# Order and pairing of the GLA output products in a one-core decoder step

## The chip, the cores and the metric

The kernel runs on one core of one Trainium2 chip. The metric is the device time of one execution in microseconds. A core has five engines that matter here: PE (TensorE, matmuls; its weight loads are shown as PEld), ACT (ScalarE), DVE (VectorE), POOL (GpSimd) and SP (SyncE, which here only issues DMAs). Each engine works through its own queue in order, and the engines wait for one another through semaphores.

## What is computed

One decoder layer for a prompt of 512 tokens and 8 sequences of 4 sample tokens, all in fp32: a gated linear attention (GLA) group and a sliding-window attention group side by side, one output projection, a layer norm, a mixture of 32 experts (top 4), a second layer norm. The part that matters here is the output of GLA, which the reference computes by chunks:

```
def step(S, inp):
    qi, ki, vi, gi = inp
    b = jnp.cumsum(gi, axis=2)
    b_last = b[:, :, -1:, :]
    o_inter = jnp.einsum('bhtd,bhde->bhte', qi * jnp.exp(b), S)
    diff = jnp.where(causal[:, :, None], b[:, :, :, None, :] - b[:, :, None, :, :], -jnp.inf)
    att = jnp.einsum('bhtd,bhtsd,bhsd->bhts', qi, jnp.exp(diff), ki)
    o = o_inter + jnp.einsum('bhts,bhse->bhte', att, vi)
    ...
o_gla = rms_norm_f32(o_gla, gla_norm_g) * jax.nn.silu(o_gate ...)
mix = jnp.concatenate([o_gla, o_swa], axis=-1) @ w_out
x1 = layer_norm(DEEPNORM_ALPHA * x + mix, ln1_g, ln1_b)
```

There are 4 heads with keys of 64 and values of 128. The output of a chunk is the sum of the scores times the values (within the chunk) and of the decayed queries times the state that the chunks before left.

## The kernel before

The tokens lie in five tiles: tiles 0 to 3 are 128 prompt tokens each (the kernel's chunk is a tile), tile 4 holds the 32 sample tokens. The stages follow one another: projections, attention, the seven "levels" that build the GLA score matrices attT (L1010 on PE, L2097 on DVE), the chunk states (L1030 and L2122), the GLA outputs, their normalisation and gating, the mixer transposes and the output projection (L1116, L1120), layer norm and routing, and then the 32 experts (L1205, L1208), whose weights stream through a ring of 16 slots.

PSUM is used as four units of two banks each. Every intermediate result has a name and a unit (ORDER), and a name can be written only after the name before it on the same unit has been freed. For the stage of the change: go0 (the output of tile 0) is on unit 0, go1 on unit 1, go2 on unit 2, go3 on unit 0 again, go4 (the samples) on unit 3. After them mixT0 is on unit 0, mixT1 on unit 1, out0 on unit 2. The output of head h = 2a + q lies in bank q of the unit, at column a * 128.

The GLA outputs on PE (L1080 to L1097). For tiles 0 to 3 and heads 0 to 3: a product of attT with gv (128 rows, 128 columns, L1088), and for tiles 1 to 3 directly behind it the product of the queries qe with the state of the tile before (L1090), into the same place. A head's keys take 64 rows, so qe and state of heads with q = 0 are in rows 0 to 63 of the array and those with q = 1 in rows 64 to 127. The samples' last products (L1095, 32 rows and 32 columns) come after tile 3. Each fp32 matmul appears as two records in the profile.

Behind PE, ACT takes the tiles in the order 0, 1, 2, 3, 4: four squares with sums (L1656) and a root (L1660). DVE follows (norm_gate, L2165): a reciprocal (L2170), four products with the gate (L2176); then it frees the unit and raises mix_ready. PE's mix_T(0) (L741 through the helper transposes) waits for mix_ready 1 and for unit 0, which is free after norm_gate(3). ACT copies the transposes (L1368, tile mix_a), and out_product(0) (L1116) follows.

SP's queue around it: ln_b is loaded after level6, the residual rows res[:, 2:] and res of the samples after go4 (L517 to L519), since res shares its memory with gv; the weights of the first expert wait for mix_ready 5 and for all earlier output DMAs. DVE reads res first in L2198, after out0. The order on each engine is written out by hand; there is no planner.

Of the kernel before, what the change touches and what calls it, by code (L numbers as in the profile page):

```python
# [21 lines left out]
P = 128  # L22
D = 1024
KD = D // P
HALF = 512
# [4 lines left out]
PT = SEQ // P  # L30
NT = PT + 1
GH, GDK, GDV = 4, 64, 128
# [85 lines left out]
def build(nc, d):  # L118
    with ExitStack() as ctx:
        def sem(name):  # L120
            return ctx.enter_context(nc.semaphore(name))
# [7 lines left out]
        def sb(name, shape, dt=F32):  # L129
            size = 2 if dt == BF16 else 4  # L130
            for n in shape[1:]:
                size *= n
            t = nc.alloc_sbuf_tensor_at(name, shape, dt, offset=here[0])
            here[0] += (size + 31) // 32 * 32
            return t
# [56 lines left out]
        gv = sb("gv", [P, NT, 512])  # L192
# [48 lines left out]
        state = sb("state", [P, PT, 2, GDV])  # L241
# [21 lines left out]
        attT = sb("attT", [P, 16, P])  # L263
# [23 lines left out]
        qe = sb("qe", [P, 2, T])  # L287
# [68 lines left out]
        def c_(name):  # L356
            a, n = early_at[name]
            return ce[:, a:a + n]
# [11 lines left out]
        def filled(name):  # L370
            return full[USE[name][0]], USE[name][1] + 1

        def emptied(name):
            return freed[USE[name][0]], USE[name][1] + 1
# [4 lines left out]
        def s_full(name):  # L379
            return full[USE[name][0]]  # L380
# [4 lines left out]
        def bank(name):  # L385
            return unit[USE[name][0]]
# [22 lines left out]
        def s_room(name):  # L409
# [23 lines left out]
        state_ready, sstate_ready, s_read, s_decayed, rms_ready, mix_ready = (sem(n) for n in (  # L433
            "state_ready", "sstate_ready", "s_read", "s_decayed", "rms_ready", "mix_ready"))
# [44 lines left out]
        def _(sp):  # L479
# [3 lines left out]
            for n in range(NIN):  # L483
# [14 lines left out]
                if 1 <= n <= 3:  # L498
                    i = n + 1
# [15 lines left out]
            sp.wait_ge(*filled("level6"))  # L515
            sp.dma_start(ln_b[:], d["ln1_b"].partition_broadcast(P)).then_inc(ln_in, 16)
            sp.wait_ge(*filled("go4"))  # L517
            sp.dma_start(res[:, 2:PT], d["x_prompt"][0, 2 * P:SEQ].rearrange("(i p) d -> p i d", p=P)).then_inc(res_in, 16)
            sp.dma_start(res[:NS, PT], d["x_sample"].rearrange("n t d -> (n t) d")).then_inc(res_in, 16)  # L519

# [210 lines left out]
        def _(pe):  # L731
            mm, tr = nc.tensor.matmul, nc.tensor.transpose
# [257 lines left out]
            for i in range(NT):  # L990
                name = f"qkT{i // 2}"
# [3 lines left out]
                for c in range(4):  # L995
                    at = i % 2 * HALF + c * r
                    ins = tr(bank(name)[:, at:at + r], qk[:r, i, c * P:(c + 1) * P], ident[:r, :r])
# [36 lines left out]
            def sample_out(a, q):  # L1034
                return bank("go4")[:NS, q * HALF + a * GDV:q * HALF + (a + 1) * GDV]
# [41 lines left out]
            level(5)  # L1077
            level(6)
            pe.wait_ge(att_ready, 1)
            for i in range(PT):  # L1080
                name = f"go{i}"
                pe.wait_ge(*emptied(name))
                if i:
                    pe.wait_ge(state_ready, i)
                for h in range(GH):
                    a, q = divmod(h, 2)
                    out = bank(name)[:, q * HALF + a * GDV:q * HALF + (a + 1) * GDV]
                    ins = mm(out, attT[:, q * 8 + a * PT + i], gv[:, i, h * GDV:(h + 1) * GDV], start=True, stop=i == 0)  # L1088
                    if i:
                        ins = mm(out, qe[64 * q:64 * q + 64, a, i * P:(i + 1) * P], state[64 * q:64 * q + 64, i - 1, a],  # L1090
                                 start=False, stop=True)
                ins.then_inc(s_full(name), 1)
            for h in range(GH):
                a, q = divmod(h, 2)
                ins = mm(sample_out(a, q), attS[:, q * 2 + a], gv[:NS, PT, h * GDV:(h + 1) * GDV], start=False,  # L1095
                         stop=a == 1)
            ins.then_inc(s_full("go4"), 1)  # L1097

            def mix_T(i):
                def src(k):  # L1100
                    return (og[:rows(i), i, k * P:(k + 1) * P] if k < 4
                            else qkv[:rows(i), i, (k - 4) * P:(k - 3) * P])
                pe.wait_ge(mix_ready, i + 1)
                if i == PT:
                    pe.wait_ge(selo, 1)
                transposes(f"mixT{i}", src, i)
# [54 lines left out]
            for b in range(PT):  # L1161
                ins = mm(bank("pos")[:, (b + 1) * NE:NT * NE].rearrange("p (t e) -> p t e", e=NE), c_("ones"),
                         msk[:, b:b + 1].to_broadcast([P, PT - b, NE]), start=False, stop=b == PT - 1)
            ins.then_inc(s_full("pos"), 1)
            pe.wait_ge(*emptied("count"))
            for i in range(NT):
                ins = mm(bank("count")[:NE, 0:1], msk[:, i], c_("ones")[:, 0:1], start=i == 0, stop=i == NT - 1)
# [164 lines left out]
            with pe.If(n_extra > 0):  # L1332
                with pe.Fori(0, MAXEXTRA) as j:
                    with pe.If(j < n_extra):
# [3 lines left out]
                        for k in range(KD):  # L1338
                            ins = tr(px[:, k * P:(k + 1) * P], xg[:, k * P:(k + 1) * P], ident)
# [3 lines left out]
                        for a, (out, lhs) in enumerate(((pg, xeTx), (pu, xeTx), (pd, heTx))):  # L1343
                            if a == 2:
                                pe.wait_ge(v_dve, j * 4 + 4)
                                for k in range(KD):
                                    ins = tr(px[:, k * P:(k + 1) * P], hbx[:, k * P:(k + 1) * P], ident)
# [3 lines left out]
                            for h in range(2):  # L1351
# [3 lines left out]
                                for k in range(KD):  # L1355
                                    ins = mm(out[:, cols], lhs[:, k], raw_x[:, k, cols], start=a == 2 and k == 0,
                                             stop=k == KD - 1)
# [1194 lines left out]
```

## Time and profile before

| | us |
|---|---|
| median of 3 runs | 1500.42 |
| lowest, highest | 1498.47, 1500.81 |
| the profiled execution | 1500.29 |
| its span, first to last instruction | 1498.1 |
| PE busy in the span | 1410.9 (94%) |
| DVE busy | 471.2 (31%) |
| ACT busy | 322.8 (22%) |
| mean granted TensorE clock | 0.952 |

Times in the rows are in us from the span's start. An engine is called busy while an instruction of it runs; records of PE may overlap, so a group's mean duration is longer than the step from one start to the next. The granted clock is a share of 2.4 GHz: 1.00 is 2.4 GHz and 0.50 is 1.2 GHz. The chain of waits is followed back from the last instruction, at each step to what released it.

### The profile page before, as it was taken

Reading aid. Unit: us, or ns where it says so; the run is one execution under the profiler, and the core shown is the slowest. Engines: PE = TensorE matmul, PEld = TensorE weight load, DVE = VectorE, ACT = ScalarE, POOL = GpSimd, SP = SyncE. Lnnn points to the kernel's source line nnn. Section 1 sums busy time; section 2 is a strip of 40 time slices with the busy share of each in tenths; the row PEclk is TensorE's granted clock in tenths of the full one; section 3 lists DMA queues with packets and bytes.
Section 4 is the critical chain, followed back from the end, with each engine's and each line's share of the span. In section 5 each row is a group of like instructions: output and inputs, shape, how many; then the busy total and the mean of one; then the engine's idle time right before and its main releaser. Section 6 shows DMA issues by size and latency. Waiting matters only on the chain.

```text
span 1498.1 us, 37690 instructions
## 1 busy us (share of the span) xinstructions
PE 1410.9 (94%) x16570; PEld 962.2 (64%) x16570; DVE 471.2 (31%) x895; ACT 322.8 (22%) x662; POOL 115.8 (8%) x119
## 2 busy tenths in 40 slices
PE   6999967998899999999999999999999999999991
PEld 5777756555566666666666666666666666666660
DVE  3235546237432222222223223222222222222223
ACT  3544453203111111112111111111111111121114
POOL 1022000000110100000100000001000000000000
PEclk8999986698799999999999999999999999999996
DMA  7211050426699999999999999999999999999944
GB/s 239 87 47 57 1 187 24 157 123 236 247 377 388 399 390 392 402 398 399 397 387 399 396 392 399 397 400 400 392 391 399 390 395 399 399 398 399 384 183 141
DMA packets 78468, 463.93 MB, mean 310 GB/s; under 512 B 12400, under 2 KB 13632, under 8 KB 29008
## 3 DMA queue, kind: packets, MB, share of 16 engines
q1 hardware_dynamic: 67616, 429.54, 72.0%
q0 software_dynamic: 10192, 31.31, 8.2%
q8 instruction: 132, 2.16, 0.6%
q10 hardware_dynamic: 512, 0.79, 0.1%
q14 instruction: 16, 0.13, 0.0%
HBM read 444.70 MB, written 22.22 MB: 312 GB/s over the span
## 4 chain that ended last, share of the span: by engine, by line
PE 87%; DVE 4%; ACT 3%; PEld 2%; DMA 2%; issue 2%; DVEq 0%; POOL 0%; PEldq 0%; SPq 0%; ACTq 0%; POOLq 0%
PE unit L1205 41%; PE unit L1208 26%; PE unit L1116 4%; PE unit L1188 2%; PE unit L1193 2%; PE unit L746 1%; PE unit L748 1%; PE unit L747 1%; PE unit L741 1%; PE unit L1010 1%; DMA xbuf<-x_prompt_dram 1%; PE unit L1088 1%; DVE attT L2097 1%; PE unit L1090 1%; PEld unit L898 1%
## 5 line engine op out<-in xcount | busy, mean ns | idle before, releaser
L1205 PE MATMUL unit<-ring_b,xeT 128*32 128x512 f32 (+1 forms) x3168 | 354.5, 489 | 1.1 <-ACT xeT L1368 1.1
L1208 PE MATMUL unit<-ring_b,xeT 128*32 128x256 f32 x1584 | 355.0, 382 | 0.0
L1208 PE MATMUL unit<-ring_a,xeT 128*32 128x256 f32 x1488 | 330.7, 379 | 0.0
L1205 PE MATMUL unit<-ring_a,xeT 128*32 128x256 f32 (+1 forms) x2976 | 330.2, 486 | 0.0
L1208 PEld LDWEIGHTS unit<-ring_b,xeT 128*32 128x32 f32 x1584 | 171.7, 110 | 56.5 <-issue 1.2
L1208 PEld LDWEIGHTS unit<-ring_a,xeT 128*32 128x32 f32 x1488 | 161.8, 110 | 52.5
L1208 PE MATMUL unit<-ring_a,heT 128*32 128x256 f32 x768 | 169.7, 379 | 0.0
L1205 PE MATMUL unit<-ring_a,heT 128*32 128x512 f32 (+1 forms) x1536 | 169.4, 486 | 0.0
L1205 PEld LDWEIGHTS unit<-ring_b,xeT 128*32 128x32 f32 x3168 | 126.8, 110 | 60.9 <-issue 5.0
L1208 PE MATMUL unit<-ring_b,heT 128*32 128x256 f32 x720 | 160.3, 379 | 0.0
L1205 PE MATMUL unit<-ring_b,heT 128*32 128x256 f32 (+1 forms) x1440 | 160.1, 486 | 0.0
L1205 PEld LDWEIGHTS unit<-ring_a,xeT 128*32 128x32 f32 x2976 | 120.2, 110 | 51.7 <-issue 2.5
L1368 ACT ACTIVATE heT<-unit 128x768 f32<-128x768 f32 x31 | 25.2, 812 | 509.7 <-PE unit L1193 509.7
L2373 DVE TENSOR_TENSOR hb<-unit,brow 128x768 f32<-128x768 f32 x32 | 30.7, 958 | 305.0 <-PE unit L1208 305.0
L2343 DVE TENSOR_TENSOR gm<-unit,brow 128x768 f32<-128x768 f32 x32 | 30.7, 958 | 234.8 <-PE unit L1208 234.8
L1208 PEld LDWEIGHTS unit<-ring_a,heT 128*32 128x32 f32 x768 | 84.3, 110 | 27.1
L683 POOL DMA_INDIRECT acc_rows<-ysb,idx x32 | 46.6, 1456 | 683.8 <-ACT ysb L1753 672.6
L1208 PEld LDWEIGHTS unit<-ring_b,heT 128*32 128x32 f32 x720 | 79.2, 110 | 25.4
L1749 ACT ACTIVATE ysb<-unit,gcol 96x768 f32<-96x768 f32 x32 | 28.7, 898 | 250.2 <-PE unit L1208 250.2
L1205 PEld LDWEIGHTS unit<-ring_a,heT 128*32 128x32 f32 x1536 | 62.9, 110 | 28.9 <-issue 0.9
L1205 PEld LDWEIGHTS unit<-ring_b,heT 128*32 128x32 f32 x1440 | 59.2, 110 | 27.9
L2273 DVE TENSOR_TENSOR row_part<-unit,ck 96x3 f32<-96x3 f32 x32 | 5.0, 156 | 209.4 <-PE unit L1182 209.4
(319 smaller groups left out, 1635.0 us busy)
## 6 DMA issues: line engine op xcount, KB each, us to landing
ring_b<-w_gate_dram SPq DMA_DIRECT2D x68, 1024.0 KB
ring_a<-w_down_dram SPq DMA_DIRECT2D x68, 1024.0 KB
ring_b<-w_up_dram SPq DMA_DIRECT2D x64, 1024.0 KB
ring_a<-w_up_dram SPq DMA_DIRECT2D x64, 1024.0 KB
ring_a<-w_gate_dram SPq DMA_DIRECT2D x60, 1024.0 KB
ring_b<-w_down_dram SPq DMA_DIRECT2D x60, 1024.0 KB
raw_a<-w_in_dram SPq DMA_DIRECT2D x16, 512.0 KB, 3.6
wo<-w_out_dram SPq DMA_DIRECT2D x4, 1024.0 KB, 12.3
```

The source lines that it names most:

```text
L683: return pool.indirect_dma_start(acc_dram, bass.IndirectOffsetOnAxis(ap=at, axis=0), out, None, compute_op=ALU.add)
L741: ins = tr(bank(name)[:, k * r:(k + 1) * r], src(k), ident[:r, :r])
L746: mm(out, xh, wh, start=start, stop=False)
L1116: ins = mm(bank(name)[:, h * HALF:(h + 1) * HALF], mix[i % 2][:, k], wo[:, k, h * HALF:(h + 1) * HALF], start=k == 0, stop=k == KD - 1)
L1188: ins = tr(px[:, k * P:k * P + CAP], half, ident[:CAP, :CAP])
L1193: ins = tr(px[:, k * P:(k + 1) * P], gm[:, k * P:(k + 1) * P], ident)
L1205: return mm(out[j * NS:(j + 1) * NS, a:b], stat(j), w[:, a:b], start=first, stop=last)
L1208: return mm(out[CAP:P, j * 256:(j + 1) * 256], stat(j), w[:, FOLD:D], start=start, stop=stop)
L1368: copy = lambda out, src, scale=1.0: nc.scalar.activation(out, src, ACT.Copy, scale=scale)
L1749: nc.scalar.activation(ysb[:CAP, 0:FOLD], pd[:CAP, 0:FOLD], ACT.Identity, scale=gcol[:CAP, par:par + 1])
L2343: tt(gm[:], pg[:, 0:FOLD], brow[:, 0], ALU.add).then_inc(h_part, 1)
L2373: tt(hb[:], pu[:, 0:FOLD], brow[:, 1], ALU.add).then_inc(h_part, 1)
```

## The change

The outputs of a tile are split into two functions. within_chunk(i) does the four score products of a tile, bank by bank (q outside, a inside), with start only for the first product of a bank. from_state(i) does the four state products, with q inside, so that the two row halves alternate. PE runs within_chunk of tiles 0, 1 and 2, then the samples' products, then from_state(1) and (2), then within_chunk(3) and from_state(3). SP waits for go3 as well before it loads res[:, 2:].

```diff
             sp.wait_ge(*filled("go4"))
+            sp.wait_ge(*filled("go3"))
             sp.dma_start(res[:, 2:PT], d["x_prompt"][0, 2 * P:SEQ].rearrange("(i p) d -> p i d", p=P)).then_inc(res_in, 16)
...
             pe.wait_ge(att_ready, 1)
-            for i in range(PT):
-                name = f"go{i}"
-                pe.wait_ge(*emptied(name))
-                if i:
-                    pe.wait_ge(state_ready, i)
-                for h in range(GH):
-                    a, q = divmod(h, 2)
-                    out = bank(name)[:, q * HALF + a * GDV:q * HALF + (a + 1) * GDV]
-                    ins = mm(out, attT[:, q * 8 + a * PT + i], gv[:, i, h * GDV:(h + 1) * GDV], start=True, stop=i == 0)
-                    if i:
-                        ins = mm(out, qe[64 * q:64 * q + 64, a, i * P:(i + 1) * P], state[64 * q:64 * q + 64, i - 1, a],
-                                 start=False, stop=True)
-                ins.then_inc(s_full(name), 1)
+            def head_out(i, a, q):
+                return bank(f"go{i}")[:, q * HALF + a * GDV:q * HALF + (a + 1) * GDV]
+
+            def within_chunk(i):
+                pe.wait_ge(*emptied(f"go{i}"))
+                for q in range(2):
+                    for a in range(2):
+                        h = 2 * a + q
+                        ins = mm(head_out(i, a, q), attT[:, q * 8 + a * PT + i], gv[:, i, h * GDV:(h + 1) * GDV],
+                                 start=a == 0, stop=i == 0 and a == 1)
+                if i == 0:
+                    ins.then_inc(s_full("go0"), 1)
+
+            def from_state(i):
+                pe.wait_ge(state_ready, i)
+                for a in range(2):
+                    for q in range(2):
+                        ins = mm(head_out(i, a, q), qe[64 * q:64 * q + 64, a, i * P:(i + 1) * P],
+                                 state[64 * q:64 * q + 64, i - 1, a], start=False, stop=a == 1)
+                ins.then_inc(s_full(f"go{i}"), 1)
+
+            within_chunk(0)
+            within_chunk(1)
+            within_chunk(2)
             for h in range(GH):
                 a, q = divmod(h, 2)
                 ins = mm(sample_out(a, q), attS[:, q * 2 + a], gv[:NS, PT, h * GDV:(h + 1) * GDV], start=False,
                          stop=a == 1)
             ins.then_inc(s_full("go4"), 1)
+            from_state(1)
+            from_state(2)
+            within_chunk(3)
+            from_state(3)
```

## Rows read from the trace of the kernel before

**Rows 1.** The page: the chain that ended last, share of the span by engine.
```profile
PE 87%; DVE 4%; ACT 3%; PEld 2%; DMA 2%; issue 2%; DVEq 0%; POOL 0%; PEldq 0%; SPq 0%; ACTq 0%; POOLq 0%
```

**Rows 2.** Stretch, length, busy us of PE, PEld, DVE, ACT, POOL, clock, DMA, GB/s.
```profile
1000.00:1400.00 400.00, 400.00 (x5390) 267.68 (x5386) 101.54 (x179) 62.53 (x108) 30.62 (x24) 1.00 1.02 396
```

**Rows 3.** Waits of SP's queue, 380 to 1480: total us, times, longest.
```profile
SPq L532 <- PE unit L1208: 866.1, 367, 32.0
```

**Rows 4.** Chain of waits in order of time around the change: start, us, what.
```profile
264.58 2.50 PE unit L1088 x10
267.09 0.72 PE unit L1090 x2
267.81 0.72 PE unit L1088 x2
...
283.76 1.15 ACT squares L1656 x8
...
285.17 0.19 DVE ms L2170
...
286.72 0.03 DVEq L2180
...
290.04 13.87 PE unit L1116 x32
```

**Rows 5.** Busy time by stretch, columns as in rows 2: where the clock moved.
```profile
228.06:231.47 3.41, 3.41 (x29) 2.37 (x30) 3.12 (x5) 1.06 (x1) 0.00 (x0) 0.50 0.00 0
231.47:234.70 3.23, 3.23 (x60) 3.04 (x56) 2.69 (x7) 0.00 (x0) 0.00 (x0) 1.00 0.03 5
...
241.71:245.12 3.41, 0.00 (x0) 0.00 (x0) 2.80 (x6) 3.41 (x4) 0.59 (x1) 1.00 0.00 0
...
245.92:264.58 18.66, 11.62 (x112) 10.84 (x112) 8.04 (x11) 0.00 (x0) 1.17 (x1) 0.50 0.27 79
264.58:285.56 20.98, 20.98 (x64) 14.89 (x64) 4.19 (x17) 6.68 (x37) 0.00 (x0) 0.50 0.03 11
286.79:289.50 2.71, 2.71 (x13) 2.71 (x14) 1.98 (x7) 0.88 (x2) 0.00 (x0) 0.50 0.84 301
289.50:303.70 14.20, 14.20 (x37) 6.44 (x36) 0.07 (x1) 1.32 (x2) 0.00 (x0) 1.00 1.02 413
...
388.49:395.31 6.82, 5.77 (x43) 2.53 (x45) 1.13 (x1) 2.18 (x3) 2.12 (x3) 0.50 0.40 119
```

**Rows 6.** Timeline of PE: start, us from first start to last end, instruction.
```profile
230.78 0.83 PE L1048 MATMUL unit<-s,qbm 64*32 64x128 f32 x6
249.53 3.68 PE L1010 MATMUL unit<-qR,kE 64*128 64x64 f32 x32
264.58 2.50 PE L1088 MATMUL unit<-gv,attT 128*128 128x128 f32 x10 [2.80 <-DVEq L2112]
283.65 1.91 PE L1095 MATMUL unit<-gv,attS 32*32 32x128 f32 x8
```

**Rows 7.** Single lines: durations in ns (min/median/max), first and last start.
```profile
L1048 PE MATMUL unit<-s,qbm x6: 401/418/418, 230.8 to 231.2; 64*32 64x128 f32 x6
L1088 PE MATMUL unit<-gv,attT x32: 421/421/582, 264.6 to 282.6; 128*128 128x128 f32 x32
```

**Rows 8.** Timeline of all engines, tile 0's normalisation to the first transposes.
```profile
269.68 1.12 DVE L2176 SCALAR_TENSOR_TENSOR og<-unit,ms,og 128x128 f32<-128x128 f32 x4
...
272.19 0.28 ACT L1656 ACTIVATE squares<-unit 128x128 f32<-128x128 f32 x1 [2.83 <-PE unit L1090]
...
273.36 0.21 ACT L1660 ACTIVATE ms<-ms 128x4 f32<-128x4 f32 x1
...
283.76 0.28 ACT L1656 ACTIVATE squares<-unit 128x128 f32<-128x128 f32 x1 [4.41 <-PE unit L1090]
...
286.79 1.09 PE L741 MATMUL unit<-ck,og 128*128 128x128 f32 x4 [1.23 <-DVEq L2180]
```

## The prediction

> **What bounds the kernel now.** First the page's chain by engine, then the busy time of the expert stage. PE carries 87% of the chain [rows 1]. From 1000 to 1400 us, a stretch of it, PE is busy throughout [rows 2], while the weight queue on SP waits for PE to free ring slots, 866.1 us in 367 waits [rows 3]. The experts are bound by PE, not by DMA, and nothing in them is touched here: they stay as they are and start when what is before them ends. Then the chain around the change, in order of time [rows 4]. It passes without a gap through the GLA outputs: ten L1088 records (scores), then two L1090 (states) and two L1088 in turn, 0.72 us for each two; then ACT's squares and root and DVE's normalisation of tile 3, the mixer transposes L741, the output products L1116. From 264.58 to 283.74 that stage is PE's, and a granted clock of 0.50 stands over all of it [rows 5], which is 1.2 of 2.4 GHz. It rose only at 289.50. So PE is the bound, and a slow one, for two reasons besides the clock.
>
> **Reason one, the alternation.** At 1.2 GHz a back to back record of 128 columns costs 0.213 us: L1095's 8 records take 1.91 us, the last of them, like every such record, 0.42, and (1.91 - 0.42) / 7 = 0.213 [rows 6, 7]. A matmul is two records. One full alternation (two L1088, two L1090) takes 2 x 0.72 = 1.45 us [rows 4], against 4 x 0.213 = 0.85; the other 0.60 are two changes between 128 and 64 rows, 0.30 each. The stage's 64 records at 0.213 are 13.6, its 24 changes at 0.30 are 7.2: 20.8, where 20.98 is measured from the first start to L1095's end [rows 5], so the account is whole.
>
> **Reason two, one row half at a time.** L1048 has 64 rows and 128 moving columns as L1090 has, but takes both row halves in turn. Six of its records at 1.2 GHz take 0.83 us, each 0.418 long: two steps of 0.206 for three pairs [rows 6, 7]. So the halves run side by side, 0.107 a record at L1095's step. Its stationary side has 32 columns where L1090 has 128. L1010 has 128 and also goes through the halves in turn: 32 records in 3.68 us, 0.115 a record with start and end [rows 6], but only 64 moving columns. One row bounds the moving side, one the loading side; none has both wide. If loads and moving hide each other, a pair costs 0.213, and that I take, since L1088 loads 128 columns under 128 moving at (2.50 - 0.58) / 9 = 0.213 after its first record [rows 6, 7]. The other end is 0.213 a record, halves one after another.
> Here the Trainium skill (TensorE: Matmul & The Clock Gate, Part 3, "The mechanism") speaks against the change: it says that a weight load overlaps running matmuls only where the row groups differ. By that the next pair's loads would lie behind the running one, an estimated 0.32 a pair and 1.3 us more for 12 pairs; L1088 disagrees in this trace, for each of its loads uses the same rows as the matmul before it.
>
> **The change part by part**, in us of the profiled execution.
> (1) within_chunk(0), (1), (2) run back to back: 24 records, the first step longer (0.58 against 0.42 of duration), then 0.213 each; at the low clock the last starts at 269.65. The zeroing of a bank is now done by the first product in it; same instructions, no cost. Tile 0 is filled at 266.7 as before.
> (2) The samples' 8 records follow, with one change before and one behind.
> (3) from_state(1), (2): 8 pairs, no change between them. Then a change, within_chunk(3), a change, from_state(3), 4 pairs.
> Sum at the low clock: 24 changes become 4, 20 x 0.30 = 6.0 off; 24 state records go from 0.213 to 0.107, 2.6 off; 20.98 becomes 12.4. go3, filled at 283.7 now with the samples behind it, is filled at about 277.3 with the samples ahead of it.
> (4) The clock. It rose at 231.47 under L1043 and L1048, at 289.50 after 2.71 us of back to back 128x128 transposes, and at 395.31, 5.4 us after the first expert product at 389.89; neither the half-wide L1010 nor the alternation brought it [rows 5]. The change makes a back to back stretch of 128x128 products of 5.3 us. I take it that the clock rises within it or at its end, 2.7 to 5.4 us after its start, and work with 269.0. The remaining steps halve: samples until 270.5, go1 filled at 271.2, go2 at 271.7, within_chunk(3) from 271.8, go3 at 273.5. within_chunk(3) needs unit 0 free of tile 0; norm_gate(0) ends at 269.68 + 1.12 = 270.8 [rows 8], just in time, and that would be felt (under 1 us) if tile 3 stood earlier in the order.
> (5) What is late next. mix_T(0) writes unit 0, so it waits for norm_gate(3). ACT takes the tiles in order; one costs it 1.38 (272.19 to 273.57 [rows 8]) and DVE 1.55 (285.17 to 286.72 [rows 4]). Both have idled between tiles (ACT 4.41 before the last squares [rows 8]); now they queue. go1 at 271.2, ACT until 272.6, then DVE has three tiles in a row: 272.7 + 3 x 1.55 = 277.4. L741 starts at 277.4 instead of 286.79: **9.4 us** off. With a rise at 267.3 or at 270.0 the same walk gives 10.3 or 8.6.
> (6) PE's idle gap before L741 grows from 1.23 [rows 8] to 3.9 us. In 241.71 to 245.12 PE was idle throughout and the clock fell [rows 5]. If it falls here too, the transposes and ACT's copy take the same 3.15 us as now, and a late rise lets some L1116 records cost 0.86 instead of 0.43: 0 to 1.5 lost. If it stays, 16 transposes take 1.7 instead of 3.25, of which 0.85 shows, the rest being under ACT's copy of the first eight. I book zero, between the two.
> The Trainium skill (TensorE: Matmul & The Clock Gate, "Why this matters for your kernels") warns that PE gaps over about 3 us between bursts bring back the low clock. By that rule the time is up to 1.5 us over mine.
> (7) SP. The loads of res[:, 2:] and of the samples' rows must not overwrite gv, so they now wait for go3 as well: 273.5, where they waited for the samples until 285.56 (283.65 + 1.91 [rows 6]). Behind them in SP's queue stands the expert weight stream, which waits for mix_ready = 5 anyway; norm_gate(4) ends 1.5 after norm_gate(3), so it starts some 9 us earlier too. The first reader of res is L2198, which waits for out0, the 13.87 us of L1116 behind L741 [rows 4]. Cost nothing; if the stream did not move, it would only lose slack.
> (8) Behind L1116 every gate up to the experts is PE, DVE, ACT or a DMA that one of them releases; none stands at a fixed time. The 9.4 us arrive at the end.
>
> **The sum.** The profiled execution took 1500.29 (its span of 1498.1 and 2.2 around it), 0.13 under the median of 1500.42, so its differences are taken over as they are: 1500.42 - 9.4 = **1491.0**.
>
> **The rivals.**
> A, the forecast: 10.3 + 0.85 to 8.6 - 1.5 off, 1489.3 to 1493.3. 64%.
> B, the clock stays low through the stage, as now. For it: the 11.62 us of PE work on 64 and 32 rows within 245.92 to 264.58 did not raise it [rows 5]; against it: the new stretch is as dense as the transposes that did. go3 at 277.3, then ACT and DVE as now (283.74 to 286.79, 3.05): 280.35, 6.4 off, 1494.0. 15%.
> C, the halves do not run side by side where both sides are 128 wide. With a risen clock go1 comes 0.4 later and the rest hides under DVE: 1491.4, inside A. With the low clock 2.6 come on top of B: 1496.6. 5%.
> D, better than all that: under 1489.3, by an early rise and the clock's phase later on. 5%.
> E, the saving is returned before the experts. The clock is low in 388.49 to 395.31 [rows 5], under 5.4 us of the first expert product; where its rise falls can differ by one to two us either way, and only on top of B or C does that bring the result within 0.2% of now, 1497.4 and more. 8%.
> F, slower: the clock falls in the new gap and stays low under the output products. At twice its 0.43 (13.87 / 32 [rows 4]), an L1116 record loses 0.43; 9.4 + 3.0 us are lost after 29 records, some 25 us at the low clock. The longest dense run at the low clock here, from 389.89, is 5.4 us. 1503.4 and more. 3%.
>
> **How the numbers follow.** The range goes from just under A to C's end, 1488.0 to 1496.6, and leaves out about one in eight. 0.2%, 3.0 us, is about what a measurement of this kernel can tell from no change. Faster: A, B, C and D, 0.89; same 0.08; slower 0.03.
>
> **What would show it.** In the profile after: records of the score products at 0.21, then 0.11 us; four steps of 0.3 where there were 24; state records starting two by two; a rise of the clock between 267.3 and 270.0; ACT and DVE without idle time between tiles 1, 2 and 3; L741 at about 277.4; L1205 some 9 us earlier. Wrong would be: a clock of 0.50 throughout (then 1494.0), state records one by one, L741 released by something other than norm_gate(3), or a longer expert stage.

## The result and the profile after

| | before | changed |
|---|---|---|
| median, 4 runs each (us) | 1499.99 | 1491.52 |
| lowest to highest | 1498.47 to 1500.81 | 1489.86 to 1491.93 |
| profiled execution | 1500.29 | 1491.93 |
| its span | 1498.1 | 1489.8 |

The ratio is 0.9943, 95% interval 0.9927 to 0.9959: 8.5 us less, where 9.4 were forecast. A second set of four runs of the same program, taken later beside other variants, gave 1491.20 and 0.9940 (0.9924 to 0.9957).

In the changed kernel the lines have moved: scores L1091 (was L1088), states L1101 (was L1090), samples L1110 (was L1095), transposes L742, output products L1135, squares L1675, DVE's reciprocal and gating L2189 and L2195, experts L1224 and L1227. First the timeline of PE through the stage (start, us from first start to last end), which answers to rows 4 and 6:

```profile
264.61 5.49 PE L1091 MATMUL unit<-gv,attT 128*128 128x128 f32 x24 [2.80 <-DVEq L2131]
270.03 1.29 PE L1110 MATMUL unit<-gv,attS 32*32 32x128 f32 x8
271.25 1.16 PE L1101 MATMUL unit<-state,qe 64*128 64x128 f32 x16
272.34 1.16 PE L1091 MATMUL unit<-gv,attT 128*128 128x128 f32 x8
273.43 0.71 PE L1101 MATMUL unit<-state,qe 64*128 64x128 f32 x8
278.35 1.09 PE L742 MATMUL unit<-ck,og 128*128 128x128 f32 x4 [4.20 <-DVEq L2199]
```

The stage that took 20.98 us takes 9.53 (264.61 to 274.14). Then PE is idle for 4.20 us, where it was idle for 1.23 [rows 8]. The busy time by stretch shows the clock (last but two column), as rows 5 did:

```profile
270.54:274.14 3.60, 3.60 (x39) 2.95 (x37) 0.90 (x5) 2.10 (x16) 0.00 (x0) 1.00 0.00 0
274.14:277.36 3.22, 0.00 (x1) 0.00 (x0) 2.52 (x11) 2.92 (x22) 0.00 (x0) 1.00 0.56 172
277.36:278.35 0.99, 0.01 (x1) 0.04 (x1) 0.78 (x4) 0.00 (x0) 0.00 (x0) 0.50 0.97 401
278.35:284.19 5.84, 5.84 (x19) 4.45 (x20) 2.05 (x7) 2.05 (x2) 0.00 (x0) 0.50 0.55 215
```

It rose at 270.54, fell at 277.36 in the gap and rose again only at 284.19, 2.4 us into the output products. The chain of waits, which answers to rows 4, shows what the stage is bound by now:

```profile
270.10 1.22 PE unit L1110 x8
271.32 0.67 PE unit L1101 x8
272.01 1.15 ACT squares L1675 x8
...
273.42 0.19 DVE ms L2189
...
273.71 1.14 DVE og L2195 x4
...
275.07 0.19 DVE ms L2189
...
276.73 0.19 DVE ms L2189
...
278.35 3.65 PE unit L742 x16
281.99 14.89 PE unit L1135 x32
```

PE is in it only until tile 1 is filled, at 272.0; from there, behind ACT's squares of tile 1, DVE normalises three tiles in a row, 1.65 us each (273.42, 275.07, 276.73). out0 takes 14.89 where it took 13.87 [rows 4]. The expert stage is as it was, PE busy throughout and SP waiting for it, 866.4 us in 367 waits [rows 2, 3].

```profile
1000.00:1400.00 400.00, 400.00 (x5394) 267.93 (x5389) 102.43 (x179) 62.43 (x108) 30.38 (x24) 1.00 1.02 395
...
SPq L533 <- PE unit L1227: 866.4, 367, 31.0
```

### The profile page after: what moved, and what is told of

Its sections match the earlier page's. It is cut to its first block, busy times and chain, and to the rows that moved or that the text cites. A ratio compares the mean times of both kernels' runs of the same rounds, so it can differ in the third digit from the quotient of the medians.

```text
span 1489.8 us, 37688 instructions
## 1 busy us (share of the span) xinstructions
PE 1402.5 (94%) x16570; PEld 959.1 (64%) x16570; DVE 471.1 (32%) x895; ACT 322.2 (22%) x662; POOL 114.8 (8%) x119
## 4 chain that ended last, share of the span: by engine, by line
PE 87%; DVE 4%; ACT 3%; DMA 2%; PEld 2%; issue 2%; DVEq 0%; SPq 0%; POOL 0%; PEldq 0%; ACTq 0%; POOLq 0%
PE unit L1224 41%; PE unit L1227 26%; PE unit L1135 4%; PE unit L1207 2%; PE unit L1212 2%; PE unit L747 1%; PE unit L749 1%; PE unit L748 1%; PE unit L1011 1%; PE unit L742 1%; DMA xbuf<-x_prompt_dram 1%; PE unit L1153 1%; PEld unit L899 1%; DVE attT L2116 1%; PE unit L875 0%
## 5 line engine op out<-in xcount | busy, mean ns | idle before, releaser
L1224 PE MATMUL unit<-ring_b,xeT 128*32 128x512 f32 (+1 forms) x3168 | 353.9, 489 | 1.1 <-ACT xeT L1387 1.1
L1227 PE MATMUL unit<-ring_b,xeT 128*32 128x256 f32 x1584 | 354.5, 382 | 0.0
L1227 PE MATMUL unit<-ring_a,xeT 128*32 128x256 f32 x1488 | 330.7, 380 | 0.0
L1224 PE MATMUL unit<-ring_a,xeT 128*32 128x256 f32 (+1 forms) x2976 | 330.2, 486 | 0.0
L1227 PEld LDWEIGHTS unit<-ring_b,xeT 128*32 128x32 f32 x1584 | 172.0, 111 | 56.3 <-issue 1.0
L1227 PEld LDWEIGHTS unit<-ring_a,xeT 128*32 128x32 f32 x1488 | 162.2, 110 | 52.4
L1227 PE MATMUL unit<-ring_a,heT 128*32 128x256 f32 x768 | 169.7, 379 | 0.0
L1224 PE MATMUL unit<-ring_a,heT 128*32 128x512 f32 (+1 forms) x1536 | 169.4, 486 | 0.0
L1224 PEld LDWEIGHTS unit<-ring_b,xeT 128*32 128x32 f32 x3168 | 126.8, 110 | 60.4 <-issue 4.5
L1227 PE MATMUL unit<-ring_b,heT 128*32 128x256 f32 x720 | 160.3, 379 | 0.0
L1224 PE MATMUL unit<-ring_b,heT 128*32 128x256 f32 (+1 forms) x1440 | 160.1, 486 | 0.0
L1224 PEld LDWEIGHTS unit<-ring_a,xeT 128*32 128x32 f32 x2976 | 120.3, 110 | 51.4 <-issue 2.5
L1227 PEld LDWEIGHTS unit<-ring_a,heT 128*32 128x32 f32 x768 | 84.5, 110 | 27.0
L1227 PEld LDWEIGHTS unit<-ring_b,heT 128*32 128x32 f32 x720 | 79.4, 110 | 25.3
L1224 PEld LDWEIGHTS unit<-ring_a,heT 128*32 128x32 f32 x1536 | 63.0, 110 | 28.7 <-issue 0.9
L1224 PEld LDWEIGHTS unit<-ring_b,heT 128*32 128x32 f32 x1440 | 59.3, 110 | 27.8
```

The lines of the kernel that those rows point to most:

```text
L1224: return mm(out[j * NS:(j + 1) * NS, a:b], stat(j), w[:, a:b], start=first, stop=last)
L1227: return mm(out[CAP:P, j * 256:(j + 1) * 256], stat(j), w[:, FOLD:D], start=start, stop=stop)
```

## The experiments

The theory: the stage gained by fewer changes of row count, by row halves side by side and by the clock, and DVE's queue of three tiles and the gap ahead of L742 took part of it back. The rivals were that the halves do not matter, that the clock is no matter of what PE does here, and that the order (24 score records, 12 products, together, samples in between, tile 3 last) is what brings the gain. All ratios are to the kernel before on the same chip: its median was 1499.99 beside the changed kernel, 1500.48 beside the halves in blocks, tile by tile, samples last and other units, 1499.34 beside the other units with samples last or tile by tile, the doubled scores and the halves apart, 1500.06 beside the rest. So medians from different groups are compared by their ratios. The last two columns are read from each profile: from the first score product to the first mixer transpose, and to the first output product.

| kernel | median (us) | ratio (95%) | to transposes | to out0 |
|---|---|---|---|---|
| before | 1499.34 to 1500.48 | 1 | 22.2 | 25.4 |
| changed | 1491.52 | 0.9943 (0.9927 to 0.9959) | 13.7 | 17.2 |
| changed, second set | 1491.20 | 0.9940 (0.9924 to 0.9957) | 13.3 | 16.7 |
| halves in blocks | 1490.09 | 0.9932 (0.9915 to 0.9948) | 13.3 | 16.8 |
| tile by tile | 1488.65 | 0.9921 (0.9904 to 0.9937) | 11.5 | 14.7 |
| samples last | 1489.80 | 0.9930 (0.9913 to 0.9946) | 12.0 | 15.5 |
| other units | 1487.60 | 0.9915 (0.9899 to 0.9932) | 10.0 | 13.2 |
| other units, samples last | 1487.30 | 0.9917 (0.9901 to 0.9934) | 9.4 | 12.6 |
| other units, tile by tile | 1486.38 | 0.9914 (0.9898 to 0.9931) | 9.1 | 11.9 |
| the same, copy first | 1486.32 | 0.9908 (0.9892 to 0.9925) | 9.5 | 11.8 |
| other units on before | 1498.87 | 0.9992 (0.9982 to 1.0002) | 20.9 | 24.4 |
| doubled scores on before | 1497.04 (one run) | | 18.8 | 22.2 |
| halves apart | 1492.87 (one run) | | 15.2 | 18.4 |
| tile 3 early | 1492.41 (one run) | | 14.5 | 18.0 |

**Row halves in blocks.**

```diff
-                for a in range(2):
-                    for q in range(2):
+                for q in range(2):
+                    for a in range(2):
                         ins = mm(head_out(i, a, q), qe[...], state[...], start=False, stop=a == 1)
```

> The changed kernel with the state products of one row half after the other (q outside, a inside). If row halves run side by side where both sides are 128 wide (theory A), the state records stop starting in pairs: at the clock of 2.4 GHz a record then costs about 0.107 us instead of 0.053, so go1 is filled some 0.4 us later (272.4), the transposes L741 start at about 278.8 and the time is 0.4 us over the changed kernel, about 1491.9, not to be told from it by the time but by the starts. If the pairs give nothing (theory C), starts and time are as in the changed kernel, 1491.5.

The timeline of PE shows the 16 state records in 1.26 us, where the changed kernel has 1.16:

```profile
268.83 1.26 PE L1101 MATMUL unit<-state,qe 64*128 64x128 f32 x16
...
L1101 PE MATMUL unit<-state,qe x8: 272/272/373, 268.8 to 269.3; 64*128 64x128 f32 x8
```

I expected 1.7 or more (16 x 0.107) under theory A. The second row, of the single line, has 8 records starting within 0.5 us (by their starts in pairs, 0.01 us apart), although the program has four of one half and then four of the other. So this edit did not do what it was made for: the order within from_state decides nothing, PE takes up the other half over four records. The time (1490.09) is not over the changed kernel's. Whether the halves matter was still open.

**Row halves apart.** The half with q = 0 of tiles 1 and 2 is put ahead of within_chunk(3), the half with q = 1 behind it. half_state(i, q) is from_state(i) for one q alone.

```diff
...
-            from_state(1)
-            from_state(2)
-            within_chunk(3)
-            from_state(3)
+            half_state(1, 0)
+            half_state(2, 0)
+            within_chunk(3)
+            half_state(1, 1)
+            half_state(2, 1)
+            half_state(3, 1)
+            half_state(3, 0)
```

> The changed kernel, with the state products of heads with q = 0 of tiles 1 and 2 (8 records, one row half) before within_chunk(3), and those with q = 1 behind it, then tile 3. Theory A (halves run side by side, and PE finds the other half among the next few records whatever their order): with none of the other half in reach, records of one half start one by one, 0.107 to 0.11 us apart at 2.4 GHz, twice the 0.053 of the changed kernel. Rival (a 64-row record of this size costs half anyway): 0.055 apart. The time, about 1.5 us over the changed kernel through the later go1, is not the question.

Timeline of PE, then the rows of the single line in that stretch, loads and matmuls (durations in ns, first and last start):

```profile
270.33 1.16 PE L1100 MATMUL unit<-state,qe 64*128 64x128 f32 x8
...
L1100 PEld LDWEIGHTS unit<-state,qe x8: 183/188/188, 270.3 to 271.1; 64*128 64x128 f32 x8
L1100 PE MATMUL unit<-state,qe x8: 272/272/373, 270.3 to 271.2; 64*128 64x128 f32 x8
```

Eight records of one half take the 1.16 us that sixteen take in the changed kernel. With 0.272 for the last and 0.214 for the first step, (1.16 - 0.27 - 0.21) / 6 = 0.113 a record against 0.053 in pairs. In this kernel the other half always goes to another PSUM bank too, but a change of bank alone does not make pairs: the first four of the eight records go to tile 1's unit and the next four to tile 2's, and the steps stay at 0.11. Theory A holds: halves run side by side with 128 columns loaded and 128 moving, and what the program must give is records of the other half close behind, not an alternation. How close, the 16 records behind within_chunk(3) bound: twelve of q = 1, then four of q = 0. Their first nine start one by one, 0.11 us apart, and pairs (0.005 us apart) come only among the last seven. The rows also weigh against what the Trainium skill says of loads (TensorE: Matmul & The Clock Gate, Part 3, "The mechanism"), that they overlap running matmuls only where row groups differ: these loads, each 0.18 to 0.19 long at steps of 0.11, use the same half of the rows as the matmul running, and the step is no longer than that of the 128-row L1091 (0.11). The same section also lets a load run ahead into a background weight buffer; that would fit the row, and no run here shows whether it is the reason.

**Scores twice, on the kernel before.** 12 score products (24 records) whose results are overwritten go ahead of the old loop.

```diff
             pe.wait_ge(att_ready, 1)
+            for name in ("go0", "go1", "go2"):
+                pe.wait_ge(*emptied(name))
+            for n in range(3):
+                for h in range(GH):
+                    a, q = divmod(h, 2)
+                    mm(bank(f"go{n}")[...], attT[:, q * 8 + a * PT + n], gv[:, n, ...], start=True, stop=True)
```

> The kernel before with the 12 score products of tiles 0 to 2 computed once more ahead of its loop (their results are overwritten), 24 back to back records and 5.3 us more work. Theory (dense products bring the clock up, the alternation did not): the clock rises in or just behind the added stretch, an alternation of four records takes about 0.85 us instead of 1.45, the 12 of them give back about 7 us, and the transposes run high: 1497 to 1499. Rival (the clock at this place does not depend on what PE does, or falls back under the alternation): 5.3 us more, 1505.5.

Busy time by stretch, and one of the chain's pairs of records:

```profile
264.05:268.46 4.41, 4.41 (x20) 4.41 (x21) 0.00 (x0) 0.00 (x0) 0.00 (x0) 0.50 0.16 51
268.46:279.71 11.25, 11.25 (x63) 8.35 (x61) 3.91 (x15) 5.32 (x28) 0.00 (x0) 1.00 0.00 0
...
270.20 0.42 PE unit L1097 x2
```

More work, and 2.3 us less time than the kernel before on that chip (1497.04 in one run, against 1499.10 to 1499.60 in seven). The clock rises under the added dense records and stays up through 11 us of the same alternation that ran low before; a cycle of four records takes 0.83 us instead of 1.45 [rows 4]. So the alternation does not bring the rise, but it does not bring a fall either; the clock fell at 282.12, in the idle gap of 2.08 us ahead of L741. A back to back record steps by 0.112 us at 2.4 GHz (0.113 by the row of the halves apart). Of the 0.83, 4 x 0.112 = 0.45 are the records and 0.38 the two changes: a change costs 0.19 at 2.4 GHz, 0.30 at 1.2.

**Tile by tile.** The split products in the old order of tiles, samples last.

```diff
-            within_chunk(1)
-            within_chunk(2)
+            for i in range(1, PT):
+                within_chunk(i)
+                from_state(i)
             for h in range(GH):
                 ...
-            from_state(1)
-            from_state(2)
-            within_chunk(3)
-            from_state(3)
```

> The split and paired products, but tile by tile as before: scores of tile 0, then scores and states of tiles 1, 2 and 3 each, the samples last. 6 changes of row count between the tiles' products instead of 24. Theory A (what counts is when the last tile comes and how ACT and DVE queue): go1 is filled at about 269.7, DVE does not queue three tiles in a row, and with a clock that rises in the stretch L741 starts at about 276.5, some 1.5 to 2 us before the changed kernel: 1489.5. Rival (the clock rises only because 24 score records stand together): it stays at 1.2 GHz, go3 is filled at about 275.9, L741 at 278.9 and the time is 1492.

```profile
264.84 3.78 PE L1091 MATMUL unit<-gv,attT 128*128 128x128 f32 x16 [2.80 <-DVEq L2128]
268.55 1.23 PE L1101 MATMUL unit<-state,qe 64*128 64x128 f32 x8
269.71 1.17 PE L1091 MATMUL unit<-gv,attT 128*128 128x128 f32 x8
...
273.19 1.05 PE L1111 MATMUL unit<-gv,attS 32*32 32x128 f32 x8
276.33 0.85 PE L742 MATMUL unit<-ck,og 128*128 128x128 f32 x4 [2.09 <-DVEq L2196]
```

This is PE's timeline. Theory A: L742 at 276.3 (276.5 expected), 1488.65 (1489.5 expected; its interval meets the changed kernel's, so the marks in the profile are what tells them apart). Tile 1 is filled at 269.8 instead of 272.0, while PE still runs low, and the clock rises all the same (eight records of L1091 take 1.17 us, as they do high). 24 score records need not stand together, and tile 3's place needs no care: PE comes to it at 271.45, when the wait for unit 0 is over. The clock still fell, at 276.60, just behind the remaining gap of 2.09 us: out0 is 14.7 us behind the start, 3.2 behind the transposes' start.

**Samples last.** The samples' products go behind from_state(3), nothing else.

> The changed kernel with the samples' products behind tile 3. By the account of the changed kernel (go1 at 272.0 sets ACT, then three tiles of 1.65 us on DVE) go1 comes 1.1 us earlier and so does L741, at about 277.2; PE's gap before it shrinks from 4.2 to about 2 us, so the clock may stay up and out_product(0) starts high, another 1 to 2 us: 1488.5 to 1490.5. If the place of the samples does not matter: 1491.5.

```profile
268.31 1.16 PE L1101 MATMUL unit<-state,qe 64*128 64x128 f32 x16
269.73 1.16 PE L1091 MATMUL unit<-gv,attT 128*128 128x128 f32 x8 [0.25 <-DVEq L2198]
...
271.46 1.06 PE L1114 MATMUL unit<-gv,attS 32*32 32x128 f32 x8
275.41 1.09 PE L742 MATMUL unit<-ck,og 128*128 128x128 f32 x4 [2.90 <-DVEq L2199]
```

Transposes start 12.0 us after the stage does, against 13.7 and 13.3: the samples in between cost the place that they take ahead of tile 1. Now within_chunk(3) does wait for unit 0, 0.25 us. The clock fell in the gap here too. The median of 1489.80 agrees, but its interval meets that of the changed kernel; the marks in the profile are what shows it.

**Tile 3 early.** within_chunk(3) ahead of from_state(1).

> The changed kernel with within_chunk(3) ahead of from_state(1). PE reaches it at about 271.2, after tile 0's unit is free (270.8), so there is no stall; but go1 is filled 1.1 us later and with it DVE's queue of three tiles and L741: 1 us over the changed kernel, 1492.5, seen in the profile as squares of tile 1 at about 7.5 + 1.0 us after the stage's start. If norm_gate(0) came later than PE, there would be an idle stretch of PE ahead of it.

```profile
270.76 1.16 PE L1091 MATMUL unit<-gv,attT 128*128 128x128 f32 x8 [0.34 <-DVEq L2198]
271.85 1.61 PE L1101 MATMUL unit<-state,qe 64*128 64x128 f32 x24
278.95 1.08 PE L742 MATMUL unit<-ck,og 128*128 128x128 f32 x4 [5.49 <-DVEq L2199]
```

PE did stall, 0.34 us, which the expectation had at none, since here it came sooner (the clock rose 4.4 us after the stage's start, not 5.9). Tile 3's place is worth that stall and the records ahead of tile 1: transposes at 14.5 us after the start, some 1 us later.

**Other units behind the stage.** The first 20 names after go4 take their PSUM unit in another turn.

```diff
-         + [(name, n % 4) for n, name in enumerate(TAIL)]
+         + [(name, (1, 2, 0, 3)[n % 4] if n < 20 else n % 4) for n, name in enumerate(TAIL)]
```

> The changed kernel with other PSUM units for what follows: mixT0 on unit 1, mixT1 on unit 2, out0 on unit 0, and so on in that turn for the first 20 names behind go4. The first transposes then wait for norm_gate(1) and (2) instead of (3). If the remaining gap of 4.2 us is only the wait for unit 0: L741 starts at about 275.0 and 276.7, the clock stays at 2.4 GHz, L1135's successor (output product of tile 0) starts at 278.4 instead of 281.8 and loses no 1.0 us to a low clock: 4.4 us under the changed kernel, 1487.1. If the gap has another cause or is returned later: 1491.5.

```profile
273.33 0.71 PE L1101 MATMUL unit<-state,qe 64*128 64x128 f32 x8
274.94 0.63 PE L742 MATMUL unit<-ck,og 128*128 128x128 f32 x4 [0.90 <-DVEq L2199]
...
276.59 0.63 PE L742 MATMUL unit<-ck,og 128*128 128x128 f32 x4 [0.59 <-DVEq L2199]
...
278.15 14.00 PE L1135 MATMUL unit<-wo,mix_a 128*128 128x512 f32 x32 [0.50 <-DVEq L2198]
```

The gap of 4.20 us is now three of 0.90, 0.59 and 0.50, the clock holds (four transposes in 0.63 us instead of 1.09, out0 in 14.00 instead of 14.89), and the first output product starts 13.2 us after the stage does instead of 17.2. 1487.60, 1487.1 expected. The gap was the wait for unit 0. The ratios' intervals just meet (0.9932 and 0.9927); the marks do not.

**The same units, samples last.**

> The other PSUM units for what follows, and the samples' products behind tile 3. Theory (DVE's queue of three tiles, started by go1, now sets the first output product): go1 comes 1.1 us earlier than with the units alone, norm_gate(3) ends at about 277.0 and the output product of tile 0 starts there: 1 us under the kernel with the units alone, 1486.6. If ACT (squares of tiles 1 to 3 and the samples, then the copy) sets it: no gain, 1487.6.

It starts out0 at 12.6, 0.6 earlier instead of 1.1, by DVE's queue as before; the clock of this profile rose late (the 24 score records take 5.49 us, so all of them were low). The times can't be told apart, by ratio 0.9917 and 0.9915.

**The same units, tile by tile.**

> The other PSUM units, and the products tile by tile with the samples last. ACT and DVE are fed in time, so norm_gate(3) ends at about 276.3, but ACT is done with the samples' squares only at 275.9 and copies the first transposes until 277.0: output product of tile 0 at 277.0, 1.2 us under the kernel with the units alone: 1486.4. If it is the same as that one (1487.6), something else releases the product.

```profile
271.87 1.06 PE L1111 MATMUL unit<-gv,attS 32*32 32x128 f32 x8
272.85 0.66 PE L742 MATMUL unit<-ck,og 128*128 128x128 f32 x4
...
275.65 13.97 PE L1132 MATMUL unit<-wo,mix_a 128*128 128x512 f32 x32 [0.83 <-ACT mix_a L1384]
```

PE's timeline: the transposes follow the samples without a gap, and the output product is released by ACT's copy, as expected. It starts 11.9 us after the stage does, 1.3 earlier than with the units alone. The time does not show it: 1486.38 is the number expected, but the kernel before was 1.1 us faster on this chip too, and the ratios are 0.9914 and 0.9915.

**The copy ahead of the samples' squares on ACT.** The squares and root of tile 4 move behind mix_in(0).

```diff
             mix_in(0)
+            rms(PT)
             mix_in(1)
```

> Products tile by tile, the other PSUM units, and on ACT the copy of the first transposes ahead of the samples' squares and root. If ACT's order sets the first output product, it now starts when norm_gate(3) is done on DVE, about 11.2 us after the stage's start instead of 11.9: 1485.7. If not: 1486.4.

```profile
274.93 0.20 ACT L1676 ACTIVATE ms<-ms 128x4 f32<-128x4 f32 x1
275.75 1.02 ACT L1384 ACTIVATE mix_a<-unit 128x1024 f32<-128x1024 f32 x1 [0.62 <-PE unit L742]
```

No gain to be measured: 1486.32, ratio 0.9908 against 0.9914, out0 at 11.8. ACT now idles 0.62 us for the transposes, which stand behind the samples on PE; in this profile the bound has gone back to PE. But here the clock rose 5.20 us after the stage's start, against 4.34 in the profile it is compared with, and so the transposes started 0.4 us later on PE (9.5 against 9.1). What ACT's order is worth with an equal clock stays open.

**The units alone, on the kernel before.**

> The kernel before with only the other PSUM units for what follows the GLA outputs. Theory (in the kernel before PE is behind on its own work, so the wait for unit 0 is worth little): transposes start when the samples end, at 285.6, the output product of tile 0 at about 289.0 instead of 289.9: 1 us less, 1499. Rival (the units are worth the 4 us that they are worth on top of the change): 1496.

```profile
283.32 1.84 PE unit L1095 x8
285.16 3.60 PE unit L741 x16
```

The transposes follow the samples at once; out0 starts 24.4 us after the stage does instead of 25.4, as expected. In time the ratio is 0.9992 (0.9982 to 1.0002), 1.2 us less and not told from no change, but well short of the rival's 4 us. The units are worth 4 us only where PE is ahead of DVE.

**The changed kernel again**, on the chip of the tile 3 early, copy first and units on before runs.

> The changed kernel once more, beside the runs below on the same chip: 1491.5, and 1490 to 1492.5 for single runs, whose spread comes from where the clock happens to rise and fall.

1491.20, with single runs from 1490.45 to 1491.83.

## Why the prediction was right, and what was off

The mechanism held: fewer changes, halves side by side, the clock, and DVE's queue as the next bound. That the median came within 0.5 us of 1491.0 is in part luck. By the saving it was 0.9 off, 8.5 against 9.4: the sum started from 1500.42, where the four runs of the kernel before have 1499.99. And in the profile 1.0 us less than forecast was saved at L742 and 1.4 more were lost in the gap and the low clock behind it; 0.6 and 0.5 that the forecast did not have came back later.

**What bounds, and the account of the stage** were right. Two changes and four records make the cycle of 1.45, and the experiment with doubled scores separates its parts again at the other clock.

**(1) to (3)** were right as far as the clock stayed low: 24 score records in 5.49 us, as the forecast's 5.07 to the last start and 0.42 have it. Four changes are left, three of them at the high clock. One slip in the sum: 264.58 + 12.4 gives 277.0 for go3 at the low clock, not 277.3; only rival B and its 1494.0 hang on it, by 0.3 us.

**Row halves** ran side by side, 16 records in 1.16 us at 2.4 GHz, 0.053 each. I wrote this as a merit of q inside a; the experiment with blocks shows that the inner order is worth nothing and the one with halves apart that their nearness is.

**(4), the clock,** rose as forecast, but at 270.54, 5.9 us after the start, while I had 4.4 and a range of 2.7 to 5.4, so it fell outside the range. Over the profiles in which it rose in the stage, it rose 4.3 to 5.9 us after the start: 4.41 in the doubled scores' rows above, 4.32 with the samples last, 4.93 tile by tile, 5.93 in the changed kernel. In the alternation it never did [rows 5]. That moved go1 from 271.2 to 272.0 and DVE's start on tile 1 from 272.7 to 273.42. It is the first mis-sized term, 0.7 us.

**(5)** had the right engine but a tile too short: 1.65 on DVE when tiles queue, not 1.55, for between tiles 0.24 us pass where I had taken the time to the release of PE. Three tiles give 4.93 instead of 4.65, 0.3 us. L742 starts at 278.35, not 277.4.

**(6)** I booked nothing for the clock in the gap, between 0.85 gained and 1.5 lost. It fell, as the Trainium skill has it for gaps of more than about 3 us (TensorE: Matmul & The Clock Gate, "Why this matters for your kernels"); the trace agrees with 4.20 us of idle time, but the clock also fell in or just behind gaps of 2.90 (samples last), 2.09 (tile by tile) and 2.08 us (doubled scores), and held over gaps of 0.90, 0.59 and 0.50 (other units). From L742's start to out0's end 18.53 us pass (278.35 to 296.88) instead of 17.12 (286.79 to 303.91 [rows 4, 8]): 1.4 lost. It lies within the 0 to 1.5 that (6) gave, at its far end; booked at zero, it is the largest error.

**(7)** The loads of res were no matter: L519's load went out at 274.2 and landed 5.2 us later; the trace has no wait for it.

**(8)** Of the 8.44 at L742, 7.03 are left at out0's end. The first expert product starts at 382.24 instead of 389.89, 7.65 earlier: 0.4 more came in the routing between and 0.2 in the DMAs x_rows and xg (9.49 us instead of 9.73); nothing here shows why. The experts ran low for 4.35 us (to 386.59) where they had run low for 5.42, which gives another 0.5. Rival E had the place right, and the sign came out the lucky way: it added a little instead of taking. Together 8.2 of the span's 8.3.

**The rivals.** B and C fell: the clock rose in the stage in every variant's profile but that of the old order (units alone, on the kernel before), and the halves do run together. F did come to pass in its first half, the clock fell and stayed low, but for 2.4 us of out0 and not for 25. The forecast's own range of A, 1489.3 to 1493.3, holds the 1491.5.

**What I had not seen** is that the order chosen by the change is not the best one. Tile by tile feeds ACT and DVE 2 us earlier, and another turn of PSUM units takes the wait for the last tile off the transposes. With both, 1486.38 (ratio 0.9914, 0.9898 to 0.9931) is the version to keep by the profile's marks, with out0 at 11.9 us against 17.2: 13.0 us under the kernel before on the same chip, where the change alone had 8.5 on its chip. The four versions with other units (0.9908 to 0.9917) can't be told apart by time.

Still open: where exactly the rise falls from run to run. The single runs of one variant spread by 0.8 to 4 us, and the profiles show rises at different distances from the same instruction; nothing here sets it.

## What to carry to other kernels

Group products by the rows that they take in the array, as far as the consumer allows and no further: the engine behind should get its first piece early, or the time saved becomes a queue there. When a stage on PE is made shorter, look at what the next PE instruction waits for, a buffer above all, since a new idle gap costs its own length and then the low clock on what follows. A small duplicate of work put ahead of a stage is a cheap way to find out what the clock alone is worth there.

## What the hardware did that I had not expected

PE ran two row halves side by side even where the program had four records of one half before four of the other (16 records in 1.26 us against 1.16 when they alternate). But with twelve of one half ahead of four of the other, the first nine started one by one. A change of row count costs 0.30 us at 1.2 GHz and 0.19 at 2.4. And an alternation that never raised the clock in 20.98 us did not lower it in 11.25 us once it was up.
